# Second mixture layer of a hybrid encoder block: one token block's V sum by gathered rows on VectorE, all U tiles before V, and half of V's low parts split on VectorE

## The reference

```python
q = einsum('td,dhq->thq', ht, w_query).reshape(T, 8, 2, 128)
scores = einsum('thpc,hpnc->thpn', q, sub_keys)       # 2 x 128 keys per head
s_top, i_top = top_k(scores, 16)
cand = s_top[:, :, 0, :, None] + s_top[:, :, 1, None, :]   # 256 pairs per head
best, pos = top_k(cand, 16)                            # 16 experts per head, 128 per token
gates = softmax(best)
act = gelu(einsum('td,tkd->tk', h_blk, expert_u[i_blk]))
out = einsum('tk,tkd->td', act * g_blk, expert_v[i_blk])
x = layer_norm(ALPHA * x + out, ln2_gain, ln2_bias)
```

## Time and profile before

| | |
|---|---|
| runs | 2232.27, 2237.18, 2237.53 us, median 2237.18 |
| profiled execution | 2237.41 us, its span 2235.7 us |
| busy share of the span | PE 98%, PEld 79%, DVE 48%, ACT 29%, POOL 39% |
| mean granted TensorE clock | 0.963 of full speed |
| HBM | 255.56 MB read, 69.21 MB written |
| chain that ended last | PE 86%, DVE 12% |

### The profile page before, as it was taken

How to read it: one execution, slowest core, us unless ns; L and a number is a source line. 1 busy time by engine, 2 the same in 40 slices (tenths; PEclk the granted TensorE clock), 3 DMA queues, 4 the chain that set the end, 5 groups by cost and what they waited for, 6 DMA issues and landing times.

```text
span 2235.7 us, 30141 instructions
## 1 busy us (share of the span) xinstructions
PE 2198.1 (98%) x10588; PEld 1761.3 (79%) x10588; DVE 1066.0 (48%) x2397; ACT 642.3 (29%) x936; POOL 873.6 (39%) x369
## 2 busy tenths in 40 slices
PE   7999999999989999999999999999999999999998
PEld 5786556788778888878888888888888888888887
DVE  3001224111411999965555544223366656566666
ACT  4523213322143333333333333322212121211211
POOL 6432001444153444434444444453344443534441
PEclk9997569999999999999999999999999999999999
DMA  5321000233332333446666666764455554645551
GB/s 175 102 76 47 1 10 24 90 99 99 123 114 88 121 130 138 141 146 189 188 188 190 190 188 188 240 231 155 159 198 192 183 206 170 215 178 207 189 186 75
DMA packets 146354, 325.65 MB, mean 146 GB/s; under 512 B 9185, under 2 KB 74849, under 8 KB 137970
## 3 DMA queue, kind: packets, MB, share of 16 engines
q1 hardware_dynamic: 51264, 184.57, 25.0%
q10 hardware_dynamic: 95026, 140.23, 18.2%
HBM read 255.56 MB, written 69.21 MB: 145 GB/s over the span
## 4 chain that ended last, share of the span: by engine, by line
PE 86%; DVE 12%; issue 0%; ACT 0%; DMA 0%; SPq 0%; DVEq 0%; ACTq 0%
PE bank L354 25%; PE bank L356 24%; PE bank L355 24%; PE bank L615 4%; PE bank L447 2%; PE bank L469 2%; DVE cand L1144 1%; PE bank L459 1%; DVE cand L1142 1%; PE bank L484 1%; DVE ijg L1145 1%; PE bank L492 1%; PE bank L450 1%; DVE top_i L1119 1%; DVE top_i L1110 1%; DVE score L1113 1%
## 5 line engine op out<-in xcount | busy, mean ns | idle before, releaser
L333 POOL TENSOR_TENSOR w_lo<-stage,w_hi 128x1024 fp32r<-128x1024 f32 x348 | 868.1, 2512 | 1319.0 <-ACT w_hi L666 1319.0
L354 PE MATMUL bank<-x_hi,w_lo 128*128 128x512 f32 x1376 | 545.7, 397 | 8.5 <-DVE x_lo L973 5.6
L356 PE MATMUL bank<-x_hi,w_hi 128*128 128x512 f32 x1376 | 538.2, 391 | 0.0
L355 PE MATMUL bank<-x_lo,w_hi 128*128 128x512 f32 x1376 | 537.3, 390 | 0.0
L666 ACT ACTIVATE w_hi<-stage 128x1024 fp32r<-128x1024 f32 x348 | 350.9, 1043 | 577.3 <-PE bank L356 561.8
L354 PE MATMUL bank<-w_hi,wt_lo 128*128 128x512 f32 x1024 | 398.3, 389 | 0.0
L355 PE MATMUL bank<-w_lo,wt_hi 128*128 128x512 f32 x1024 | 398.3, 389 | 0.0
L356 PE MATMUL bank<-w_hi,wt_hi 128*128 128x512 f32 x1024 | 398.3, 389 | 0.0
L1200 DVE TENSOR_TENSOR acc<-acc,bank 128x512 f32<-128x512 f32 x256 | 174.9, 684 | 336.5 <-PE bank L356 336.5
L354 PEld LDWEIGHTS bank<-x_hi,w_lo 128*128 128x128 f32 x1376 | 259.6, 189 | 61.8 <-DVE x_lo L973 6.5
L356 PEld LDWEIGHTS bank<-x_hi,w_hi 128*128 128x128 f32 x1376 | 259.5, 189 | 55.6
(11 more groups left out here) (204 smaller groups left out, 1848.2 us busy)
## 6 DMA issues: line engine op xcount, KB each, us to landing
stage<-in_expert_uT SPq DMA_DIRECT2D x128, 512.0 KB, 3.5
stage<-in_expert_v SPq DMA_DIRECT2D x128, 512.0 KB, 3.5
stage<-in_mix_stream SPq DMA_DIRECT2D x84, 512.0 KB, 3.4
gates<-gate_scratch ACTq DMA_DIRECT2D x32, 1024.0 KB, 4.8
act<-activation_scratch ACTq DMA_DIRECT2D x32, 1024.0 KB, 6.9
activation_scratch<-act_out_a ACTq DMA_DIRECT2D x64, 256.0 KB, 2.5
activation_scratch<-act_out_b ACTq DMA_DIRECT2D x64, 256.0 KB, 2.4
gate_scratch<-gstage_a ACTq DMA_DIRECT2D x8, 2048.0 KB, 11.1
```

What stands on the lines that cost most here:

```text
L333: nc.gpsimd.tensor_tensor(w_lo[:, slot, 0:width], stage[:, slot % STAGE, 0:width], w_hi[:, slot, 0:width], ALU.subtract).then_inc(split_do ...
L354: mm(dst, l_lo, r_hi, start=first, stop=False)
L355: mm(dst, l_hi, r_lo, start=False, stop=False)
L356: return mm(dst, l_hi, r_hi, start=False, stop=last)
```

## The change

**U first, then V.** The 128 U tiles run first, alternating between two PSUM banks, and the 96 groups of the gate matrix (of blocks 1 to 3 only) follow the tiles 50 to 97, two a tile. All four `key_scores` stand ahead of the first tile. Then TensorE runs V tile after V tile. For each it does 18 matmuls: three blocks by two halves by three, each pair of block and half summed in a bank of its own over all 128 tiles (banks 2 to 7), so that `add_out` and `acc` are gone. The last 4 tiles are run bank by bank, so that the blocks end one after the other.

**Block 0 by gathered rows.** For each of its 128 tokens (one per partition) and its 128 picks, VectorE works out the expert's index (`eidx`) and the place of its activation in the scratch tensor (`aidx`). GpSimd issues 128 indirect DMAs that fetch one activation per token (`gather_act`, 128 x 1) and 128 that fetch one row of V per token (`gather_row`, 128 x 1024) into a ring of 4. VectorE multiplies activations by gates 16 picks at a time (`weigh_picks`) and adds row times weight to `acc0` (`add_pick`, a scalar_tensor_tensor 128 x 1024). The picks are spread over V tiles 10 to 116, 1 or 2 a tile.

**Low parts.** Of V's tiles GpSimd splits the even ones and VectorE the odd ones (`split_value`). The high parts of the weights, `wt_hi`, are now rounded by ScalarE (`round_weight`), with 384 columns for the three blocks, in a ring of 5 (`WT`).

```diff
+WT = 5
+GATHER = 4
+FIRST_GATE = 50
+GATE_SPAN = 48
+CHUNK_PICKS = 16
+FIRST_PICK = 10
+LAST_PICK = 116
...
+def picks_by(v):
+
+    return max(0, min(NPICK, (v - FIRST_PICK + 1) * NPICK // (LAST_PICK - FIRST_PICK + 1)))
...
+def on_vector(tile):
+
+    return tile >= NKEY and (tile - NKEY) % 2 == 1
...
+            def gather_act(k):
+
+                nc.gpsimd.indirect_dma_start(out=weight[:, k:k + 1], out_offset=None, in_=acts,
+                                             in_offset=bass.IndirectOffsetOnAxis(ap=aidx[:, k:k + 1], axis=0)
+                                             ).then_inc(act_got[k // CHUNK_PICKS], 16)
+
+            def gather_row(k):
+
+                if k >= GATHER:
+                    pool.wait_ge(picked, k - GATHER + 1)
+                nc.gpsimd.indirect_dma_start(out=gat[:, k % GATHER, :], out_offset=None, in_=rows,
+                                             in_offset=bass.IndirectOffsetOnAxis(ap=eidx[:, k:k + 1], axis=0)
+                                             ).then_inc(gathered[k % GATHER], 16)
+
+            acts_due, rows_due = 0, 0
+            for tile in range(2 * NKEY):
+                n, v = first_expert + tile, tile - NKEY
+                if not on_vector(tile):
+                    split_low(n, n % RING, QW)
+                if v == FIRST_PICK - 6:
+                    pool.wait_ge(eidx_ready, 1)
+                    for parity in range(2):
+                        pool.wait_ge(act_written[parity], 16 * NKEY // 2)
+                while acts_due < min(NPICK, 4 * (v - FIRST_PICK + 7), picks_by(v - 4) + 2 * CHUNK_PICKS):
+                    gather_act(acts_due)
+                    acts_due += 1
+                while rows_due < picks_by(v - 4):
+                    gather_row(rows_due)
+                    rows_due += 1
...
+            def value_part(v, b, half):
+                n = first_value + v
+                s, w = n % RING, v % WT
+                r, c = slice((b - 1) * P, b * P), slice(half * 512, half * 512 + 512)
+                return mm3(bank[2 * b + half][:], wt_hi[:, w, r], wt_lo[:, w, r], w_hi[:, s, c], w_lo[:, s, c],
+                           v == 0, v == NKEY - 1)
+
...
+            for v in range(NKEY - TAIL_TILES):
+                wait_split(pe, first_value + v)
+                pe.wait_ge(wt_done, v + 1)
+                for b in range(1, TB):
+                    for half in range(2):
+                        ins = value_part(v, b, half)
+                ins.then_inc(quarter_used, 1)
...
+            def round_weight(v):
+                sc.wait_ge(wt_mul, v + 1)
+                if v >= WT:
+                    sc.wait_ge(quarter_used, first_value + v - WT + 1)
+                act_f(wt_hi[:, v % WT, :], act[:, v // UNIT % 2, v % UNIT, :], ACT.Copy).then_inc(wt_hi_done, 1)
...
+            for v in range(1, NKEY):
+                round_weight(v)
+                if v + 3 < NKEY:
+                    ahead(first_value + v + 3)
+                if v % UNIT == 0 and v // UNIT + 1 < NUNIT:
+                    sc.wait_ge(wt_done, v)
+                    load_unit(v // UNIT + 1)
...
+            def add_pick(k):
+
+                dve.wait_ge(gathered[k % GATHER], 16 * (k // GATHER + 1))
+                if k >= 1:
+                    dve.wait_ge(picked, k)
+                v.scalar_tensor_tensor(out=acc0[:], in0=gat[:, k % GATHER, :], scalar=weight[:, k:k + 1], in1=acc0[:],
+                                       op0=ALU.mult, op1=ALU.add).then_inc(picked, 1)
...
+            def weigh(w):
...
+                a = act[:, u % 2, k, :].rearrange("p (b t) -> p b t", b=NGB)
+                v.tensor_tensor(a, a, gates[:, u % 2, :, k, :], ALU.mult).then_inc(wt_mul, 1)
+
+            def weight_low(w):
+                dve.wait_ge(wt_hi_done, w + 1)
+                v.tensor_tensor(wt_lo[:, w % WT, :], act[:, w // UNIT % 2, w % UNIT, :], wt_hi[:, w % WT, :],
+                                ALU.subtract).then_inc(wt_done, 1)
+
+            def split_value(tile):
+
+                n = first_expert + tile
+                dve.wait_ge(hi_done, n + 1)
+                v.tensor_tensor(w_lo[:, n % RING, :], stage[:, n % STAGE, :], w_hi[:, n % RING, :],
+                                ALU.subtract).then_inc(value_split, 1)
...
+            for w in range(NKEY):
+                if w + 1 < NKEY:
+                    weigh(w + 1)
+                weight_low(w)
+                if w + 3 < NKEY and on_vector(NKEY + w + 3):
+                    split_value(NKEY + w + 3)
+                if w == FIRST_PICK:
+                    dve.wait_ge(acc_ready, 1)
+                for k in range(picks_by(w - 1), picks_by(w)):
+                    if k % CHUNK_PICKS == 0:
+                        weigh_picks(k // CHUNK_PICKS)
+                    add_pick(k)
```

More of the change, by code:

```diff
@@ L112, in build @@
[L112 to L120, removed]
@@ L238, in wait_product, with wait_split @@
                 eng.wait_ge(quarter_used, 4 * STREAMED.index(name) + (r + 1 if by_column else 4))
+        def wait_split(eng, n):
+            tile = n - first_expert
+            if on_vector(tile):
+                eng.wait_ge(value_split, sum(on_vector(k) for k in range(tile + 1)))
+            else:
+                eng.wait_ge(split_done, n + 1 - sum(on_vector(k) for k in range(tile + 1)))
         block = ctx.enter_context(nc.Block())
@@ L648, in _ @@
+            pe.wait_ge(wt_done, NKEY)
+            for b in range(1, TB):
+                for half in range(2):
+                    for v in range(NKEY - TAIL_TILES, NKEY):
+                        ins = value_part(v, b, half)
+                    ins.then_inc(ffn_done, 1)
         @block.scalar
@@ L923, in _ @@
+            for t in range(NKEY):
+                if t in EXP_AT:
+                    exp_gates(EXP_AT[t])
+                if t in TURN_AT:
+                    evac_picks(TURN_AT[t])
+                gelu_tile(t)
+                ahead(first_expert + t + 4)
+                store_tile(t)
+                for g in range(groups_by(t - 1), groups_by(t)):
+                    evac_group(g)
+                if t == last_group_tile + 2:
                     for half in range(2):
@@ L961, in _ @@
+            for t in range(1, TB):
+                normalize(t)
         @block.vector
@@ L1195, in add_out @@
-            def add_out(u, m):
-                t, half = divmod(m, 2)
-                c = slice(half * 512, half * 512 + 512)
-                dve.wait_ge(acc_done, u * 8 + (m + 1))
-                dve.wait_ge(ffn_done, u * 8 + (m + 9))
-                v.tensor_tensor(acc[:, t, c], acc[:, t, c], bank[4 + m % 4][:], ALU.add).then_inc(acc_done, 1)
-            def unit_out(u, w):
-                for m in range(8):
-                    add_out(u, m)
-                    if w is not None and 2 <= m < 2 + UNIT:
-                        if m == 2:
-                            dve.wait_ge(ffn_done, u * 8 + 8)
-                        weigh(u + 1, m - 2, w)
@@ L1211, in _ @@
[L1211 to L1225 removed]
+                share = grec.unsqueeze(2).broadcast_to(heads)
@@ new lines, in _, with by_pair @@
+            for t in range(1, TB):
+                first_level(t)
+                finish_gates(t - 1)
+                second_level(t)
+                if t >= 2:
+                    split_gates(t - 1)
+                decode(t)
+            finish_gates(TB - 1)
+            step(v.tensor_copy(iota_g[:], iota_n[:].unsqueeze(2).broadcast_to([P, NKEY, 2])))
+            pairs = [P, GT // 2, NKEY, 2]
+            keys_of = iota_g[:].unsqueeze(1).broadcast_to(pairs)
+            def by_pair(values):
+                return values.rearrange("p (b t) -> p b t", t=2).unsqueeze(2).broadcast_to(pairs)
@@ new lines, in _ @@
+            for t in range(1, TB):
+                for half in range(2):
+                    c = slice(half * 512, half * 512 + 512)
+                    dve.wait_ge(ffn_done, 2 * (t - 1) + half + 1)
+                    ins = v.scalar_tensor_tensor(out=x1[:, t, c], in0=x1[:, t, c], scalar=ALPHA, in1=bank[2 * t + half][:],
+                                                 op0=ALU.mult, op1=ALU.add)
+                step(ins)
+                norm_stats(x1[:, t, :], t).then_inc(ln2_var, 1)
+                norm_apply(x1[:, t, :], t, ln_g2, ln_b2, ln2_var, ln2_sqrt, y_ready)
```

554 lines of the change are left out of this document (241 added, 313 removed).

## The result

The changed kernel takes **2442.5 us** (median of 4 runs, 2438.25 to 2445.09) where the kernel before takes 2237.03 beside it (2232.27 to 2237.53). The ratio is 1.0922, with a 95% interval of 1.09 to 1.0944: 9% slower. The forecast was 2349 us, slower, for the reason that the runs confirm, and 94 us too low: 205 us are lost where 112 were forecast. The profiled execution has a span of 2443.1 us.

What follows compares the result with a forecast made beforehand. TensorE bound the old kernel; sparing it 201 us gives a 2034.7 us span, but a four-engine loop in V adds turns of 14.2 us: 1557.4 + 736.4 + 44.9 + 8.2, plus 1.7 around, 2349 us; range 2235 to 2480.

Steps and rivals of the forecast that it cites:

- What TensorE is spared: TensorE's removed block-0 V matmuls, gate groups and pick waits: 201 us less, span 2034.7 us if nothing else bound it.
- The loop: V part: VectorE, ScalarE, GpSimd and gathers wait in a circle; rows cannot be requested before VectorE begins their tile.
- the turn: One pass of the four-engine wait circle in V, serving two tiles: 14.2 us against 8.16 at TensorE's pace.
- c: GpSimd's time to issue one indirect DMA, taken as 1.0 us between 0.34 to 0.39 and 2.37.
- L: Time for a gathered 512 KB row transfer to land after its issue, taken as 3.5 us.
- the start: Early V: GpSimd begins near 1503.5, first row landed at 1555, TensorE can begin tile 11 at 1557.
- the formula: Time per two V tiles: the longer of 8.5 + 2.2c + L and 6.1 + 4.6c + L, 14.2 us.
- the longer path: Larger of two sums per two V tiles, through the first or second tile's rows; both gave 14.2 us.
- Rival 1: V part: picks keep TensorE's pace and transfers bind next, 4.53 us a tile, 2085 us; faster altogether 0.13.
- Its small form: V part: VectorE and GpSimd wait for each other's SBUF access, some 18 us if no idle time hides it.
- Rival 2: V part: TensorE's clock falls to 1.2 GHz, 16.3 us a pair, 2477 us; this or c above 1.4: 0.12.
- the one sign that might have gone wrong: U part: waits of TensorE there would mean VectorE's picks came late, counting against the forecast.

Runs made afterwards that it cites:

- cut by moving the subtractions: Changed kernel with all low parts of V made by VectorE, none by GpSimd: 2095.2 us, ratio 0.9369.
- tightened: Changed kernel with all low parts of V made by GpSimd, none by VectorE: 2930.73 us, ratio 1.3104.
- the kernels with the loop open: Changed kernel, V's low parts all on VectorE: 2095.2 us; plus 8 gathered-row places, requests four tiles earlier: 2093.47; plus first pick six tiles later: 2077.43.
- the last window: V-part profile of changed kernel with VectorE low parts, 8 gathered-row places, requests four tiles earlier, first pick at tile 16: 2077.43 us median, 2063.47 profiled.
- the ring of 8: Changed kernel with 8 gathered-row places, requests four tiles earlier: 2149.23 us with low parts shared, 2093.47 with all on VectorE.
- two blocks: Changed kernel with block 3's V matmuls left out of all but the last 4 tiles: 2432.72 us, ratio 1.0878.

## Why the prediction was right in kind and 94 us too low

**What TensorE is spared: right.** 2036.4 us forecast, 2035.87 measured without picks. The end of U came 1.3 us early. No wait of TensorE for picks is left.

**The loop: right, and shown.** Cut by an earlier request it gives back 260 us, cut by moving the subtractions 347 us; tightened it costs 488 us more. What was wrong is the size of two terms of the turn, c and L, and through them the start. "Cannot be requested before VectorE has begun tile w" is what each turn of the timeline shows.

**"I take 1.0, near the geometric middle": too low.** c is 1.25. The instruction itself takes 0.94; what I hadn't counted is a gap of 0.30 us before the next. It enters 4.6 times: 1.15 us a turn.

**"A row gather is 512 KB in the same 4 KB pieces: 3.5": too low.** 3.76 from the issue's end in the turn above, 0.26 us a turn, and more in most. The Trainium skill (DMA: Bandwidth & Descriptors, "Anatomy of one DMA — SWDGE (gpsimd) path") would have had, as an estimate by its formula, 3.2 us for 512 KB and 2.3 for 128 KB, a fixed 2.0 and the bytes over 436 GB/s. From the issue's end these runs show 3.92 and 2.07 in the median, so the small one about agrees and the large one takes 0.7 us longer.

With c = 1.25 and the L of that turn the formula gives 6.1 + 4.6 x 1.25 + 3.76 = 15.6 while activations are fetched (measured 15.8), and without their issues 8.5 + 1.0 x 1.25 + 3.76 = 13.5, one row an even tile (measured 14.2). Against the forecast, 39 turns by 1.4 and 13 by 0.5 are 61 us of the turns' 79. Most of the other 18 or so is again **L**. For the row that a turn waits for last, the time from the issue's end to the add has a mean of 4.25 us (4.14 while activations are fetched, 4.58 afterwards), 0.49 above 3.76, or 25 us over 52 turns. The formula's other terms are some 0.2 us a turn too long (no gap lies between an issue and its own landing, and adds start 1.20 apart and not 1.28), 12 us, which leaves 13 of the 18. The longest landings, 6.28 and 6.22 us, stand in the two longest turns (20.27 and 20.08). In the first the row's issue ends at 1599.35, and ScalarE's loads of the next unit, 768 KB each, go out at 1599.50 and 1599.85. The DMA share is then 0.92:

```profile
1599.50:1605.60 6.10, 5.96 (x18) 4.44 (x18) 1.28 (x1) 1.00 (x2) 0.00 (x0) 0.72 0.92 332
```

That I averaged the picks to 1.2 a tile, where they come as 1 or 2, is no part of the 18. Summed turn by turn with the picks of `picks_by`, at c = 1.25 and L = 3.76, the longer path has a mean of 15.5 us while activations are fetched and 13.6 afterwards, the same as the average (15.6 and 13.5). At the forecast's own c and L it would have been worth 6 us. A turn with one pick in each tile takes 14.5 us (subtractions at 1939.60 and 1954.13), one with a second pick in a tile 17.3 to 17.7 (1954.13 to 1971.41, 1907.45 to 1925.10).

**The start: 14 us late.** The first add is at 1568.62 and not at 1555. GpSimd began where the forecast had it (1503.87), but its 33 activations and one row cost 1.25 and not 1.0 each (8 us), and some took up to 1.91 us beside VectorE's work. 14 + 79 us are the 94 within some 2 us.

**Rival 1, picks at TensorE's pace**, wasn't the changed kernel's case. Its price, 2085 us, stands beside the measured 2077 to 2095 of the kernels with the loop open, but that is partly luck. It used 341 GB/s at full use, where the last window has 358 at 0.97, or 369; with that its sum would be 4.17 us a tile, 10 us above 2036. And what filled first with the ring of 8 was GpSimd with its issues. Its small form, VectorE and GpSimd in each other's way, cost nothing in V while the loop left VectorE idle at the right moments. The price was paid as soon as an experiment shortened the loop.

**Rival 2, the clock**, happened in part and cost nothing. In the turn above TensorE has been idle for 4.11 us when it starts at 1903.91. Up to 1907.40 its matmuls start 0.43 us apart at a granted clock of 0.51 (1.2 GHz), from there to 1913.80 0.23 apart at 1.00 (2.4 GHz). With two blocks the clock fell further and the time did not rise.

**In the U part**, the one sign that might have gone wrong: VectorE's `oh_gate` (L1218) takes 0.775 us in the mean, with 2.635 as its longest, because it falls together with GpSimd's subtractions (three of them take 3.31 us from 1101.84, with a subtraction from 1102.07, and 1.08 us from 1105.74, with none). VectorE had room, and TensorE never waited for it.

## What to carry to other kernels

A lead that is counted in tiles is a lead in time only if the requesting engine can run ahead. Here the requester stood in program order behind a subtraction, released at last by the very engine that consumes the request, so a lead of four tiles was worth nothing, and one number (`v - 4` to `v - 2`) decided between 9% slower and 2% faster. Walk every request backwards to what releases it, add up the closed loop, and compare that with the pace of the engine it serves; take a transfer's time with the other loads that run beside it, and expect that opening the loop brings up the next bound, here GpSimd's own issues and, close behind, the DMA engines.

## What the runs showed of the hardware

- An issue of an indirect DMA by GpSimd isn't free of VectorE. It takes 0.94 us alone, and up to 2.98 us beside an unbroken row of VectorE instructions with two SBUF inputs (`L373` in the kernel with all low parts on VectorE: least 0.933, median 1.424, most 2.976). Which of these VectorE instructions do it wasn't tried one by one. The Trainium skill (SBUF — State Buffer, section "Who interferes with whom") has such VectorE instructions contend with GpSimd instructions that read SBUF, and only infers that descriptor generation is spared; here it is not.
- The same sharing goes both ways between long instructions: 2.39 to 4.42 us for GpSimd's subtraction, 1.28 to 3.90 for VectorE's add.
- What an indirect issue costs on its engine doesn't depend on its size: 0.95 us for 4 bytes a partition, 0.94 for 4 KB, and 0.30 between two.
- The landing of such a gather, 512 KB in 4 KB pieces, isn't one number: from the issue's end to the add that waits for it 3.07 to 6.28 us in the changed kernel.
